# First two up blocks of each MLP chunk by seven block products

## The reference, cut to what matters

```python
def sqrelu_mlp(h, w_up, w_down):     # w_up (2048, 8192), w_down (8192, 2048)
    u = jax.nn.relu(h @ w_up)
    return (u * u) @ w_down

for layer in range(DEPTH):           # DEPTH = 2
    h = rmsnorm(x, norm_mix_w[layer]);  x = x + mixer(h)
    h = rmsnorm(x, norm_mlp_w[layer]);  x = x + sqrelu_mlp(h, mlp_w_up[layer], mlp_w_down[layer])
return rmsnorm(x, final_norm_w)
```

## Time and profile before

| | us |
|---|---|
| median of 3 runs (1993.83 to 1995.13) | 1994.04 |
| the profiled execution | 1995.09 |
| its span, first to last instruction | 1993.3 |
| TensorE busy, 9089 matmuls | 1984.1 |
| VectorE busy | 1581.1 |
| ScalarE busy | 1066.0 |

### The profile page before, as it was taken

How to read it: one execution, slowest core, us unless ns; L and a number is a source line. 1 busy time by engine, 2 the same in 40 slices (tenths; PEclk the granted TensorE clock), 3 DMA queues, 4 the chain that set the end, 5 groups by cost and what they waited for, 6 DMA issues and landing times.

```text
span 1993.3 us, 25055 instructions
## 1 busy us (share of the span) xinstructions
PE 1984.1 (100%) x9089; PEld 1638.8 (82%) x9089; DVE 1581.1 (79%) x2190; ACT 1066.0 (53%) x1402; POOL 45.1 (2%) x55
## 2 busy tenths in 40 slices
PE   9999999999999999999999999999999999999998
PEld 7888888888888888888888878888888888888887
DVE  6777678989769868976889887989858876985875
ACT  6665665555445545544545566555445544544554
POOL 1110110000000000000000000000000000000000
PEclk9999999999999999999999999999999999999999
DMA  8556545655665475556655545564575555466563
GB/s 306 177 182 205 181 165 203 202 172 192 217 199 170 168 249 182 184 206 190 211 190 186 174 154 165 182 197 152 197 247 191 188 206 189 148 218 226 187 205 112
DMA packets 191758, 382.50 MB, mean 192 GB/s; under 512 B 6328, under 2 KB 7616, under 8 KB 191552
## 3 DMA queue, kind: packets, MB, share of 16 engines
q1 hardware_dynamic: 190288, 377.51, 56.5%
q0 software_dynamic: 1216, 3.88, 0.6%
q10 hardware_dynamic: 176, 0.07, 0.0%
HBM read 379.34 MB, written 2.10 MB: 191 GB/s over the span
## 4 chain that ended last, share of the span: by engine, by line
PE 98%; DVE 1%; issue 0%; ACT 0%; DMA 0%; ACTq 0%
PE acc L1399 26%; PE acc L1400 26%; PE acc L1401 26%; PE bank L1399 3%; PE bank L1400 3%; PE bank L1401 3%; PE acc L1426 1%; PE acc L1425 1%; PE acc L1427 1%; DVE area L1219 1%; PE bank L1427 1%; PE bank L1425 1%; PE bank L1426 1%; PE bank L1515 0%; PE bank L1592 0%; PE bank L1616 0%
## 5 line engine op out<-in xcount | busy, mean ns | idle before, releaser
L976 DVE TENSOR_TENSOR w_lo<-raw,w_hi 128x1024 fp32r<-128x1024 f32 x744 | 899.8, 1223 | 354.4 <-ACT w_hi L733 350.1
L733 ACT ACTIVATE w_hi<-raw 128x1024 fp32r<-128x1024 f32 x744 | 777.2, 1059 | 716.7 <-PE acc L1401 562.4
L1399 PE MATMUL acc<-w_hi,a_hi 128*128 128x512 f32 x1552 | 607.1, 391 | 0.0
L1401 PE MATMUL acc<-w_hi,a_lo 128*128 128x512 f32 x1552 | 604.1, 389 | 0.0
L1400 PE MATMUL acc<-w_lo,a_hi 128*128 128x512 f32 x1552 | 604.0, 389 | 0.0
L1399 PEld LDWEIGHTS acc<-w_hi,a_hi 128*128 128x128 f32 x1552 | 291.5, 188 | 61.2 <-issue 0.9
L1401 PEld LDWEIGHTS acc<-w_hi,a_lo 128*128 128x128 f32 x1552 | 291.4, 188 | 60.8
L1400 PEld LDWEIGHTS acc<-w_lo,a_hi 128*128 128x128 f32 x1552 | 291.4, 188 | 59.9
L1399 PE MATMUL acc<-w_hi,b_hi 128*128 128x512 f32 x784 | 305.7, 390 | 0.0
L1400 PE MATMUL acc<-w_lo,b_hi 128*128 128x512 f32 x784 | 305.3, 389 | 0.0
L1401 PE MATMUL acc<-w_hi,b_lo 128*128 128x512 f32 x784 | 305.0, 389 | 0.0
(11 more groups left out here) (240 smaller groups left out, 1296.8 us busy)
## 6 DMA issues: line engine op xcount, KB each, us to landing
raw<-in_mlp_w_up SPq DMA_DIRECT2D x128, 1024.0 KB, 5.4
raw<-in_mlp_w_down SPq DMA_DIRECT2D x128, 1024.0 KB, 5.1
raw<-in_hyb_w_in SPq DMA_DIRECT2D x44, 1024.0 KB, 5.3
raw<-in_attn_w_qkv SPq DMA_DIRECT2D x20, 1024.0 KB, 5.1
raw<-in_hyb_w_out SPq DMA_DIRECT2D x16, 1024.0 KB, 5.2
raw<-in_attn_w_out SPq DMA_DIRECT2D x16, 1024.0 KB, 5.1
raw<-in_hyb_w_in SPq DMA_DIRECT2D x5, 512.0 KB, 9.6
out_y<-x SPq DMA_DIRECT2D x4, 512.0 KB, 3.0
```

What stands on the lines that cost most here:

```text
L733: nc.scalar.activation(w_hi[:, ring(b, h)], raw[:, q, 2 * e:2 * e + 2, :], ACT.Copy).then_inc(hi_ready, 2 if what == ("R", HALVES - 1) else 1)
L976: nc.vector.tensor_tensor(w_lo[:, ring(b, h)], raw[:, q, 2 * e:2 * e + 2, :], w_hi[:, ring(b, h)].bitcast(F32), ALU.subtract).then_inc(lo_ ...
L1399: nc.tensor.matmul(a, xh, wh, start=first, stop=False, skip_group_check=joins)
L1401: ins = nc.tensor.matmul(a, xl, wh, start=False, stop=last, skip_group_check=joins)
```

## The change

The first two up blocks of every chunk (UP0 and UP1, 8 pairs in all) are done as a pair, by the same seven products over the first four row tiles; the steps after the products are in another order (UP_STEPS), so that the left block ends five steps before the right one, whose L6 and L7 come before R4. Weaving of the up blocks goes. The token sums (add_up_tokens, up_tokens, up_tokens_rest) are taken once per MLP, from a_hi + a_lo of the first res block, in the slot two before the MLP; their high and low parts are made again for each chunk, since s_hi and s_lo are shared with the down pairs. The partial results have no residual to go to: add_part copies them into tiles of their own (part_l, part_r), sum_pair adds what the accumulators hold at the end, and relu and square are done in these tiles.

The left block of the pair is still turned by 16 quadrant transposes of VectorE. The right one, the other two up blocks and the last res block ahead of an MLP go another way: ScalarE squares (or copies, move_res) 16 pieces of 32 partitions x 256 into the tile shifted, each to the partitions where it is wanted, and VectorE turns the four parts of it by transposes over 128 partitions (turn_shifted). Their steps are set by the tables SQUARES_..., RES_AT and turn_at. The last res block's sums of squares, mean_square, root and inverse move from steps 1 to 5 to steps 10 to 13 of the next slot, and TensorE waits for its turned form before L6.

```diff
+BY_QUADRANT = {"res"} | DIRECT
+BY_VECTOR = BY_QUADRANT | {"up"}
+QUADRANTS_UP = {3: 4, 4: 4, 6: 4, 7: 4}
+SQUARES_UP0 = {2: 2}
+SQUARES_UP1 = {1: 2, 2: 4, 4: 4, 5: 4, 6: 2}
+SQUARES_AT = {0: 4, 1: 6, 2: 6}
+SQUARES_PAIR = {3: 2, 4: 2, 5: 2, 6: 2, 7: 2, 8: 2, 9: 2, 10: 2}
+RES_AT = {2: 1, 3: 3, 4: 1, 5: 1, 6: 1, 7: 4, 8: 1, 9: 4}
+LAST_SUMS_AT = 10
...
+UP0 = {m + PERIOD * c for m in (MLP0, MLP1) for c in range(CHUNKS)}
+UP1 = {b + 1 for b in UP0}
+DOWN0 = {m + PERIOD * c + COLS + 2 * n for m in (MLP0, MLP1) for c in range(PAIR_CHUNKS) for n in range(2)}
+PAIRS0, PAIRS1 = UP0 | DOWN0, UP1 | DOWN1
+MIXED = [("P", 1), ("L", 2), ("P", 5), ("L", 3), ("P", 2), ("P", 6), ("P", 4), ("L", 4), ("P", 7),
+         ("L", 5), ("P", 3), ("R", 2), ("R", 3)]
+DOWN_STEPS = MIXED + [("R", 4), ("R", 5), ("R", 6), ("R", 7), (None, 0), ("L", 6), ("L", 7)]
+UP_STEPS = MIXED + [("L", 6), ("L", 7), (None, 0), ("R", 4), ("R", 5), ("R", 6), ("R", 7)]
...
 def late(b):
-    if b + 1 in FIRST_PAIRS:
+    if b + 1 in FIRST_PAIRS or b + 1 in (MLP0, MLP1):
         return 1
     if b in PAIRS1 and b + 1 in PAIRS0:
         return STEP_OF["R", 3]
+    if b in UP0 | UP1 or b - 1 in UP1:
+        return 1
...
 def out_at(kind, b):
+    if before_mlp(b):
+        return max(squares_at(b)) + 1
+    if kind == "up":
+        return max(QUADRANTS_UP) + 1 if b in UP0 else max(squares_at(b)) + 2
+    return max(quadrants_at(kind, b)) + 1 if kind in BY_QUADRANT else TURN_AT[kind] + 1 + late(b)
+def turn_at(kind, b):
+    return out_at(kind, b) - (kind == "up")
...
 # ScalarE
+            def squares(slot, k):
...
+                src = up_stage(b).rearrange("p t (k f c) -> p t k f c", k=COLS, f=QUADRANTS)
+                for n in range(done, done + at[k]):
+                    a, f = divmod(n, QUADRANTS)
+                    ins = nc.scalar.activation(shifted[f * QUAD:(f + 1) * QUAD, a], src[a * QUAD:(a + 1) * QUAD, :, :, f, :],
+                                               ACT.Square)
...
+            def move_res(slot, k, j):      # the same from x, with ACT.Copy
...
+            def up_tokens(slot):
+                act.wait_ge(up_added, 1 if slot.b < MLP1 - 1 else 2)
+                nc.scalar.activation(s_hi[:, :, :, :], s_up[:, :, :, :], ACT.Copy).then_inc(up_hi, 1)
...
 # VectorE
             def add_part(slot, k):
+                        if b in UP0:
+                            ins = nc.vector.tensor_copy((part_l, part_r)[side][:, tt, :], accumulator(right, src))
...
+            def sum_pair(slot, b):
+                for tt in range(TT):
+                    nc.vector.tensor_tensor(part[:, tt, :], part[:, tt, :], accumulator(b, tt),
+                                            ALU.add).then_inc(pair_summed, 1)
...
+            def add_up_tokens(slot):
+                link(nc.vector.tensor_tensor(whole, a_hi[:, 0:4, :].bitcast(F32), a_lo[:, 0:4, :].bitcast(F32), ALU.add))
+                link(nc.vector.tensor_tensor(s1, a21, a22, ALU.add))
+                nc.vector.tensor_tensor(s3, a11, a21, ALU.subtract)
+                link(nc.vector.tensor_tensor(s2, s1, a11, ALU.subtract))
+                nc.vector.tensor_tensor(s4, a12, s2, ALU.subtract).then_inc(up_added, 1)
+            def up_tokens_rest(slot):
+                dve.wait_ge(up_hi, slot.ups(1))
+                nc.vector.tensor_tensor(s_lo[:, :, :, :], s_up[:, :, :, :], s_hi[:, :, :, :].bitcast(F32),
+                                        ALU.subtract).then_inc(up_lo, 1)
...
+            def turn_shifted(slot, k, kind):
+                dst = turn.rearrange("p m (k t a c) -> p t (m k) a c", k=2, t=TT, a=QUADRANTS)
+                for a in range(QUADRANTS):
+                    ins = nc.vector.transpose(dst[:, :, :, a, :], shifted[:, a])
+                ins.then_inc(turned, 2)
...
             def post(slot, k):
+                if slot.b - 2 in UP0 | UP1:
+                    behind(Slot(slot.b - 1, slot.i), NSTEP[slot.b - 1] + k)
+                behind(slot, k)
+                if slot.b in PAIRS0:
+                    add_part(slot, k)
+                if slot.b + 2 in (MLP0, MLP1) and k == 6:
+                    add_up_tokens(slot)
+                if (slot.b + 1 in (MLP0, MLP1) and k == 2) or (slot.b in DOWN0 - FIRST_PAIRS and k == STEP_OF["R", 3] + 1):
+                    up_tokens_rest(slot)
...
-                if k == 3 and kind == "res" and j == COLS - 1:
+                if kind == "res" and j == COLS - 1 and k == (LAST_SUMS_AT + 1 if before_mlp(b) else 3):
                     mean_square(next_norm(b), slot.count(N_SUMS, 0, TT * COLS))
...
 # TensorE
-                    if b in FIRST_PAIRS and k == LAST_TURNED_AT:
+                    if (b in FIRST_PAIRS and what == ("R", 6)) or (b in (MLP0, MLP1) and what == ("L", 6)):
                         pe.wait_ge(turned_out, slot.count(N_TURNED, 0, INIT_HALVES))
```

More of the change, by code:

```diff
@@ L125, with pair_of, unit_free, side_block @@
 SUM_COUNT = {5: 1, 7: 2, 6: 3, 4: 4}
-LAST_TURNED_AT = STEP_OF["R", 6]
+def pair_of(b):
+    first = b if b in PAIRS0 else b - 1
+    steps, units = (UP_STEPS, UP_UNITS) if first in UP0 else (DOWN_STEPS, DOWN_UNITS)
+    return first, steps, steps.index((None, 0)), units
+def unit_free(b, n):
+    _, steps, _, units = pair_of(b)
+    if n < 2:
+        return STEP_OF["P", 4 if n == 0 else 3] + 1
+    side, g = units[n]
+    return steps.index((side, 2 * g + 1)) + 1
+def side_block(b, side):
+    first = pair_of(b)[0]
+    return first + (side == ("R" if first in UP0 else "L"))
+LEFT = {side_block(b, "L"): (b in DOWN0 and b not in FIRST_PAIRS) for b in PAIRS0}
 WOVEN = ({MIX_OUT0, QKV0, ATT_OUT0}
          | {m + COLS * n for m in (MLP0, MLP1) for n in range(2 * CHUNKS)}) - PAIRS0
-NSTEP = [PAIR_SPLIT if b in PAIRS0 else len(PAIR_STEPS) - PAIR_SPLIT if b in PAIRS1 else HALVES
+NSTEP = [pair_of(b)[2] if b in PAIRS0 else len(pair_of(b)[1]) - pair_of(b)[2] if b in PAIRS1 else HALVES
          for b in range(NBLK)]
 STEP0 = [sum(NSTEP[:b]) for b in range(NBLK + 1)]
+def banks_of_blocks():
+    out, last = [], 1
+    for b in range(NBLK):
+        if b not in LEFT and not (b in DOWN0 and b not in FIRST_PAIRS):
+            last = 1 - last
+        out.append(last)
+    return out
+ACC_OF = banks_of_blocks()
 def ring(b, k):
@@ L148, in pair_step, with counts @@
 def pair_step(b, k):
[L150 to L154, removed]
+    if b not in PAIRS0 | PAIRS1:
+        return None
+    _, steps, split, _ = pair_of(b)
+    return steps[k + (split if b in PAIRS1 else 0)]
+def counts(b, k):
+    return 2 if b in PAIRS0 and k == NSTEP[b] - 1 else 1
 def weight_at(b, k):
@@ L162, in weight_at @@
     side, h = what
-    first = b if b in PAIRS0 else b - 1
+    first, _, _, units = pair_of(b)
     if side == "P":
@@ L240 @@
 SUMS_AT = {1: 0, 2: 1, 4: 2, 5: 3}
+N_PAIR_SUMS = [TT * sum(p < b for p in UP0 | UP1) for b in range(NBLK + 1)]
 N_EVAC_ACT = total(BY_ACT, TT)
@@ L272, in pairs, with ups @@
     def pairs(self, per, n, b=None):
-        return self.plus(per * sum(p < (self.b if b is None else b) for p in PAIRS0) + n, 2 * per)
+        return self.plus(per * sum(p < (self.b if b is None else b) for p in PAIRS0) + n, 3 * per)
+    def ups(self, n):
+        return self.plus(sum(p < self.b for p in UP0) + n, 1)
     def chunks(self, per, n):
@@ L762, in leave @@
                 b = slot.b - 1
-                act.wait_ge(half_used, slot.halves(late(b)))
+                if b not in UP0 | UP1:
+                    act.wait_ge(half_used, slot.halves(late(b)))
                 if b > 0 and BLOCKS[b - 1][0] in DIRECT:
@@ L1194, in turn_quadrants @@
             def turn_quadrants(slot, k, kind, j):
-                at = {tick + late(slot.b - 1): n for tick, n in quadrants_at(kind, slot.b - 1).items()}
+                at = quadrants_at(kind, slot.b - 1)
                 if k not in at:
@@ L1386, in products @@
                     side, h = what
[L1387 to L1388 removed]
+                    b = side_block(slot.b, side)
+                    begins = what == MIXED[1]
                 joins = what is not None
```

219 lines of the change are left out of this document (149 added, 70 removed).

## The result

The changed kernel takes 2006.32 us (median of 4 runs, 2004.98 to 2008.33) against 1993.93 us for the kernel before: a ratio of 1.0062, 95% interval 1.0044 to 1.0079. The forecast was 1998.9 in a range of 1987 to 2005. The sign was right; the loss is 12.4 us where 4.9 were forecast.

A forecast was written before the change was run, and what follows sets the result against it. TensorE, busy 100% of the span, was taken as the bound. Pairs -8.2, MLP 0's head +5.1, MLP 1's +7.9, sum +4.8: 1999.9 us for the profiled execution, 1998.9 as median; range 1987 to 2005.

The forecast's parts named there:

- L6: Left block's plain step in the pair, waiting for the last residual block; forecast wait 2.7 us in each MLP's first pair.
- A pair gains 1.02 us: Up pair against two plain up blocks, 42.50 against 43.52 us as in down pairs; eight pairs gain 8.2 us.
- VectorE's mean load stays: Over a chunk, 36 fewer transposes save VectorE 15.7 us and added work costs about 15.2; ScalarE rises from 53% to 65%.
- The wide transpose: VectorE's transpose over 128 partitions, taken at 0.44 us like the narrow; other end 1.74, which would mean past 2010 us.
- The heads: First up pair of each MLP, where added VectorE work makes TensorE wait: 5.1 us in MLP 0, 7.9 in MLP 1.
- L2: Plain weight step (12 matmuls) early in the first up pair; forecast wait 0.2 us in MLP 0, 0.9 in MLP 1.
- P6: Product step (6 matmuls) in the first up pair, queued on VectorE; forecast wait 1.1 us in each MLP.
- the token sums' 2.6 us: Five adds on VectorE ahead of each MLP's first up pair, mostly waiting for each other, delaying the queue behind them.
- I charge nothing here: First down pairs in steady chunks: ScalarE's added small squares cost no time, every step being ready.
- The 0.35: Assumed spacing in us of ScalarE's unscaled 32x256 squares back to back.
- rival (b): ScalarE's small squares delay six first down pairs, 3 us each at 0.50 us spacing, 18 in all, 2017; chance 0.14 with another rival.
- 1.7 us of margin: Third block's preparation done at 20.1 us, first down pair starting at 21.8; 0.1 us a square, so waits from 0.45.

The follow-up runs named there:

- the first experiment: The changed kernel with four plain up blocks kept in the first chunk of each MLP, up pairs in the other three chunks; 1991.07 us, ratio to before 0.9984.
- the three fences of squares above: Three-pair kernels with closer squares: as is; output in the partitions read; whole rows read, other partitions written. Squares 0.428, 0.31, 0.428 us apart; 1988.20, 1989.26, 1987.89 us.
- the closer order: Right block's small squares one step closer, third up block's exit one step earlier; 1988.20 us without first-chunk pairs, 2002.91 us on the changed kernel with all eight.

## Why the prediction was wrong

**Right.** A pair gains 1.02 us, eight gain 8.2: measured 42.51 us for a pair, and 86.02 to the next down pair where nothing waits. VectorE's mean load stays (77% for 79%), ScalarE goes to 62% (65% forecast). The wide transpose costs no more than the narrow: 411 ns, below the 0.44 taken; the end at 1.74 was far off. The heads: MLP 0 5.7 for 5.1, with L2 0.36 (0.2), L3 0.23 (0.5), P6 0.94 (1.1), P4 0.24 (0.3), L4 0.67 (0.3), L6 2.49 (2.7). MLP 1 10.2 for 7.9: 2.7 ahead of the pair (2.2), then L2 0.71 (0.9), L3 0.28 (0.4), P6 0.97 (1.1), P4 0.23 (0.3), L4 0.66 (0.3), L6 2.34 (2.7), and 1.5 us of slow matmuls behind a wait, a cost I had not charged to any wait. In both heads TensorE loses 0.1 us at each restart beside the wait itself. Dropping the first chunk's pairs confirms the whole term. One piece of its working was too coarse: I had the token sums' 2.6 us delay all that follows, and they delay little but the entry.

L6's wait in MLP 0 has the chain that was forecast. The load of weights takes 5.4 us; its high half starts 25.4 us after the entry (24.5), VectorE makes its low half and only then turns the residual block, and the last low half of that block ends at 31.7 (31.25):

```profile
406.25 5.39 DMA raw<-in_mlp_w_up
```

```profile
411.66 1.06 ACT L832 ACTIVATE w_hi<-raw 128x1024 fp32r<-128x1024 f32 x1 [0.81 <-DMA raw<-in_mlp_w_up]
...
412.75 1.23 DVE L1134 TENSOR_TENSOR w_lo<-raw,w_hi 128x1024 fp32r<-128x1024 f32 x1 [2.14 <-ACT w_hi L832]
413.89 1.42 DVE L1432 STREAM_TRANSPOSE turn<-area 128x256 f32<-128x256 f32 x4
416.29 1.68 DVE L1229 SCALAR_TENSOR_TENSOR a_lo<-turn,vecs,a_hi 128x256 fp32r<-128x256 f32 x4 [0.97 <-ACT a_hi L843]
```

ScalarE's moves of the residual end at 410.85, before the load has landed, so they are not what L6 waits for. Ahead of it VectorE has no gap from 378.97 to 399.4, which fits the waits up to P4. This is read from one trace; no run took the residual's moves or the order behind the load away by itself.

**Wrong, and the step that failed.** "I charge nothing here: with the squares 0.35 to 0.42 apart every step is ready." The small squares are 0.428 us apart, outside that span, and six first down pairs lose 0.84 us each, 5.1 in all. The 0.35 was taken from 128-partition instructions that overlap by 0.07 to 0.1 us; these never do, since each writes to another group of 32 partitions than the one before. With 0.31 us the loss is nil in all four places behind a pair. The mechanism was named, as rival (b); its size was off (0.84 us at each pair, where it had 3), and so was its threshold. (b) put the point from which TensorE waits at 0.45: 1.7 us of margin over the third block's 16 squares. It left out the right block's 16 (the 32 of its price are those of the third and the fourth block). They delay the right block's transposes and its split, and the third block's exit stands behind that split. Over 32 squares the same margin is 0.05 us each, an estimated threshold of 0.40; nothing was run between 0.31 and 0.428. ScalarE and VectorE of the first experiment in a chunk with a pair, where TensorE enters the fourth block at 620.30 and the first down pair starts at 642.39:

```profile
618.30 0.84 ACT L909 ACTIVATE area<-area 32x256 f32<-32x256 f32 x2
619.16 1.06 ACT L834 ACTIVATE w_hi<-raw 128x1024 fp32r<-128x1024 f32 x1
...
620.26 1.23 DVE L1136 TENSOR_TENSOR w_lo<-raw,w_hi 128x1024 fp32r<-128x1024 f32 x1 [1.67 <-ACT w_hi L834]
621.40 1.42 DVE L1436 STREAM_TRANSPOSE turn<-area 128x256 f32<-128x256 f32 x4
...
622.85 1.16 ACT L842 ACTIVATE b_hi<-turn 128x512 fp32r<-128x512 f32 x2 [1.29 <-DVE turn L1436]
623.91 1.05 ACT L834 ACTIVATE w_hi<-raw 128x1024 fp32r<-128x1024 f32 x1
624.86 1.25 ACT L889 ACTIVATE stage<-acc,rinv 128x512 f32<-128x512 f32 x2
...
632.59 2.54 ACT L909 ACTIVATE area<-stage 32x256 f32<-32x256 f32 x6
...
637.40 1.42 DVE L1436 STREAM_TRANSPOSE turn<-area 128x256 f32<-128x256 f32 x4
...
640.98 1.29 DVE L1227 TENSOR_TENSOR b_lo<-turn,b_hi 128x512 fp32r<-128x512 f32 x2
```

The delay is handed back and forth: the right block's last squares (618.30) stand before a high half, VectorE waits 1.67 us for it before its low half, the transposes come behind that, the split (622.85) behind them and the third block's exit (624.86) behind the split. The third block's squares end at 635.13, 14.8 us after TensorE's entry where (b) had 12.6: 16 x 0.08 = 1.2 of the difference is their own pitch, and the rest I put down to the split, which begins only 2.5 us in. The low half ends at 642.27, and TensorE wanted it at 642.06. The forecast was too low by 5.1 us for the first down pairs, 2.9 for the heads, and 0.4 at the entry.

The Trainium skill ("VectorE: DVE Perf Modes", section "Two Vector instructions with no wait between them") states that a Vector instruction whose input or output starts in another group of 32 partitions than the one before starts only when all earlier ones have ended. VectorE's rows agree: narrow transposes 0.44 us apart with 0.436 each, wide ones 411 ns each and four in 1.42, 0.34 apart. It states it of VectorE alone; the three fences of squares above show the same on ScalarE, for the output. The Trainium skill ("ScalarE: Activation LUTs", section "What ACT_TABLE_LOAD costs") has instructions back to back overlap by about 93 ns, among figures for tiles of 128 partitions and without that condition; the row with unchanged partitions agrees (0.31 apart with 0.40 each), the row with changing ones does not.

## What to carry to other kernels

A mean load of 62% says nothing of a queue: lay the two engines' timelines of the changed stretch over each other and look for the last stretch without a gap, because all that enters it delays what ends it. When many small instructions replace a few wide ones, price their pitch, not their duration, and by a row with the same pattern of partitions. An edit that saves at every repetition but costs at the entry should be left out at the entry: here six pairs in place of eight, with one block's squares a step closer and the next block's exit a step earlier, turn 12 us of loss into 6 us of gain.

## What the runs showed that I had not expected

- ScalarE's small instructions lose 0.1 us each when the output moves to another 32 partitions (0.41 to 0.43 against 0.31 us apart).
- A wait of TensorE of 2.2 to 2.6 us was followed by about eight matmuls at the 1.2 GHz level, 1.5 us more, in some places and not in others: behind 2.34 us in MLP 1 and not behind 2.49 in MLP 0; with the token sums left out the other way about; with the closer order and all eight pairs behind 2.39 in MLP 0 and not behind 2.64 in MLP 1; with doubled squares behind one of two waits of 2.42. So the length of the wait alone does not decide it. What does stays open.
- The 2.4 us by which two executions differ at the entry to MLP 0 (386.24 and, with the block ahead of the first down pair squared wide, 383.85) all lie in the first 24 us. In the later one a wait for a DMA is 0.7 us longer and some seven matmuls start 0.43 us apart; in the other none do. A difference of 2 us between single executions can come from there.
- A loop's branch cost VectorE 3.9 + 1.5 us of idle time, with instructions being fetched, and the chunk 5.7 us: in MLP 1 and not in MLP 0, and in one of fourteen variants of nearly the same code. Why in that one stays open.
